# Another written-out order for the steady turns of a two-stream RWKV scan phase: pair products first, transposes between the inversion levels

## The chip, the cores and the metric

The kernel runs on one core of one Trainium2 chip. The metric is the device time of one launch in microseconds (us). In the trace PE is TensorE (matrix multiplies), PEld its weight loads, DVE is VectorE, ACT is ScalarE, POOL is GpSimd, SP is SyncE, which only issues transfers here. A "matmul" below is one MATMUL record of the trace; a float32 product leaves two of them, a transpose leaves one.

## The reference

Two layers of a trunk run over 512 latent and 256 context tokens of width 1024. The part of it that the change touches is the bidirectional RWKV-7 time mixing, for 16 heads of 64 channels and both directions:

```
z = h @ W_in                                   # r, k, v, low-rank decay and rate, gates
k_d, decay_d, kk * a_d  for d in (forward, backward)
for each token (context first, then latent, from the context's final state):
    S = S * w_t - (S @ kk_t) kka_t^T + v_t k_t^T
    y_t = S @ r_t                              # directions are summed
out = (norm(y) + bonus) * g
```

The second layer needs no output for the context tokens, so its scan computes y for 512 tokens only. The convolution branch, the gating unit, the merge and the feed-forward part follow, and the change leaves them alone.

## The kernel before

The scan is computed in chunks of 64 tokens (12 chunks). Two heads, 128 channels, make a pair; there are 8 pairs in each layer. Within a pair, a chunk's step is a set of small products with the inverse of a 64x64 triangular matrix, one for each chunk, head and direction.

`pair_phase(l)` exists once for each engine. It is software-pipelined in turns `t` = 0 to 9 (`KT` is 8). In turn `t` three pairs are in work at once:

* the dense work of pair `t`: the projections of k, r and v (`ktiles`, L1058, 48 products of 128x128 by 512 or 256 columns; half 0 is 512 wide, half 1 is 256 wide), the low-rank decay and rate (`up_group`, L1126, three groups "first", "both", "last") and the norm sums of kk (`single`, L1070);
* the scan of pair `t-1`: `scan(p)` and `side_work(p)`;
* the output part of pair `t-2`: mean, variance, gate (`single`, L1070).

On TensorE the scan of a pair is, in order: six pair products (`product`, 16 matmul records each, PROD0 to PROD5 below), the inversion, the blocks w, u and g, the `sources`, and a chain of 11 hops from chunk to chunk. The inversion has four full levels. Each level n consists of T0, T1, U0 and U1: 96 records of 32x32 each (the helper `mm64`, L1177). A fifth, smaller one follows (L5T, L5U, 96 records each). `side_work` is 13 transposes through TensorE, TR0 to TR12 (`turned`, mostly L1209, four records each).

Between these the other engines work:

* PROD0 waits for `yv`, ScalarE's copy of the previous pair's y out of the same PSUM banks (L2080). That copy also waits for `ya` (L2577, VectorE), since it overwrites what L2577 reads.
* PROD(j) with j >= 2 waits for VectorE's masking (L2618) of product j-2, as there are two pairs of banks.
* When masks 0 to 2 are done ScalarE gathers four blocks, when all six are done four more (L2020). VectorE then makes the start value of the inversion for half 0 and half 1 (L2631, L2634, transpose L2626). L1T0 and L1T1 wait for these.
* ScalarE copies each transpose out (L2001 to L2012, bk0 to bk12 below); transpose k waits for copy k-2.
* After L5T: copies t5 (ACT L2034) and t5v (DVE L2654); after L5U: x5 (ACT L2044) and x5v (DVE L2663). The first block w0 waits for both. Block w1 waits for w0's copy w0st (ACT L2050), since both use one bank; u0 waits for w0's second copy (L2054), u2 and `sources` for the later ones and for u0 to u2 copied out (ACT L2060, DVE L2669).
* ScalarE also computes the next pair's decays and norms in the same turn: kkln (L1924, a logarithm, with a table load L1722 ahead of it), vln0 and vln1 (L1897), kkexp (L1931, an exponential, after another table load), ex0, ex1 (L1939, L1942), ex2, ex3, kt0, kt1 (L1951). On VectorE: the shifts of k, r and v (L2415, L2419), the two running sums sum0 and sum1 (L2512), le (L2523), the factor products (L2397).

The program issues one fixed order of items to each engine. That order comes from `WEAVE`: for each engine, layer and turn there is a string of letters, one letter for one item. `weave(order, **streams)` takes the next item of the stream that each letter names. For TensorE `d` is the dense stream, `s` the scan, `x` the transposes. For ScalarE and VectorE `s` is the scan, `x` the copies of transposes, `t` the tail of earlier pairs, `p` all the rest. Within one stream the order is fixed; only the interleaving is in the string. All steady turns, `t` = 2 to 7 (`range(2, KT)`), of one layer share one string. Since each wait is issued in front of its item, the items behind it on the engine wait too.

SyncE issues the weight loads in its own order (`pair_loads`): each steady turn loads three chunks of 512 KB and one of 192 KB, released when the gate tile of the turn before is done.

Of the kernel before, what the change touches and what calls it, by code (L numbers as in the profile page):

```python
# [37 lines left out]
KT = D // P  # L38
# [109 lines left out]
def names_lora():  # L148
# [20 lines left out]
WEAVE = {}  # L169
# [1 line left out]
    "xxddxdxxdxsdssddddssxxsxdxdddxdxddddsdsddxsddsddsddsdsddsddsddddsdsdssdsddssdsddsdddssdssddddssddsds"  # L171
    "sssssssssssssssssssssssssssssssssssssss")) for t in (1,))
WEAVE.update((("PE", 0, t), (
    "xxdsxsdssdxxssxdxxdddxsddsdddsxddddsdxdddsdsddsddsddsddsxdsddsdddsdddsddsdsdddsdxddsdddsdsdsssssddss"
    "dsssdsssddsdssdssssssssssssssssssssssdsssssss")) for t in range(2, KT))
WEAVE.update((("PE", 0, t), (
    "dxsdsdsxssddxxsxxxdddsxxsxdddsdddddsdddsdddddsddsddddddxddddsdddsxddddssdsdddsssdsxddsdddsddsdsdsdds"
    "sdddssddddsddsssssssddssdsdsssssssssssssssssssssssssssss")) for t in (KT,))
WEAVE.update((("PE", 0, t), "dddddddsddddddddddsddddsddddddddsdddddddddsdddsddddddd") for t in (KT + 1,))
WEAVE.update((("A", 0, t), "xxxxxsspssxxxxssxsspxppppppxppppppppxppspspspssssssssssssspspspsssssss") for t in (1,))  # L180
WEAVE.update((("A", 0, t), "xxxxxsssxsssxssxxppxppxpppppppppxpppssxsppsppspsssspsssppspsppssssspssssss") for t in range(2, KT))
WEAVE.update((("A", 0, t), "sxsxsxsxxxssssxxxpxpppppxxpssxsssssspsssssssssssssssss") for t in (KT,))
WEAVE.update((("A", 0, t), "pxpppxx") for t in (KT + 1,))
WEAVE.update((("V", 0, t), "sssttttsststpssssssssssssspppspspsssspppssssspspsppsstpspsspspspsppppppsppsssssssssssssssssss") for t in (1,))
WEAVE.update((("V", 0, t), "ttssssttsstssstsssstpstsspssssspssspssssppspssppsppsssspssssppppppsppssssptstsssstsssspspstspspsstp") for t in range(2, KT))
WEAVE.update((("V", 0, t), "tsststsststsssssststsssstssspssspspspppssssptstsssppsssssssttsssssssssspsspsppspspspsssspppppp") for t in (KT,))
WEAVE.update((("V", 0, t), "tptppptpttppppppppt") for t in (KT + 1,))
WEAVE.update((("PE", 1, t), (
    "ddddxsdxxssxsddxdssxdxxddddddddsxsdxsddsddsxddsddsdsdsdsssssdsddxddsdsxddddsddssssssddsdssssssdsssss"
    "ssdssssssssssssssssssssssssss")) for t in (1,))  # L190
WEAVE.update((("PE", 1, t), (
    "xxsssdsxssxxdxxddddsxdsdxsddddsddddsddsdxsddsddsddsddxsdsxdsdssdsdsddxsddddsddsdsssddssdsssssdsssdss"
    "ssdddsssssssssssssssssssssssssss")) for t in range(2, KT))
WEAVE.update((("PE", 1, t), (
    "xsssxddxssxxsxddddxsxddsdsdsddsdddddsdssdsdssddddssdddsxsdxxsxsdddxsdddsddssssssssssssssssssssssssss"
    "sssssssssssssssssss")) for t in (KT,))
WEAVE.update((("PE", 1, t), "dddddsdddsddddsdddddddddddd") for t in (KT + 1,))
WEAVE.update((("A", 1, t), "xxxsxsxsspxssxssxpppxpppxppxpppppppppppspsxxsspssssssssssssspssssssss") for t in (1,))
WEAVE.update((("A", 1, t), "xxsssxxxsssssxxxpppxppxppppppppxxpssspxpspppsspssssssppsppspssssssssssps") for t in range(2, KT))
WEAVE.update((("A", 1, t), "xxxsssxsxsxsssxxpppppxxxssxxsssssssssssssssssssssss") for t in (KT,))  # L200
WEAVE.update((("A", 1, t), "pppxxx") for t in (KT + 1,))
WEAVE.update((("V", 1, t), "tssstttsstssssssspsspssppssssppsssspsssppstsspsspspppssspppspspsspppspssspsssssssssssssss") for t in (1,))
WEAVE.update((("V", 1, t), "tssssttstssssssststssspssssspsspspssssspsppsppspspssssssspppppppssssptspssstsssspsspsstspsspt") for t in range(2, KT))
WEAVE.update((("V", 1, t), "stssttsssttssssssssstssssssspspssssstsssstsptsssssspsppsppsssppspsssppsssssspssspspsp") for t in (KT,))
WEAVE.update((("V", 1, t), "ptppptptptppppppppp") for t in (KT + 1,))

# [3120 lines left out]
```

## Time and profile before

| | before |
|---|---|
| median of 3 runs | 4037.71 us (4033.7 to 4046.82) |
| profiled execution: its time | 4042.05 us |
| profiled execution: span of the core | 4040.2 us |
| PE busy | 3832.9 us, 95% of the span |
| DVE, ACT, POOL busy | 1684.2, 1136.4, 552.0 us |
| mean granted TensorE clock | 0.98 |
| scan phase of layer 0, steady turns | 233.45 to 884.36 us, six turns |
| scan phase of layer 1, steady turns | 2459.16 to 3070.76 us, six turns |

Times inside the span are counted from the first instruction. A turn is counted here from the end of the last hop of the pair before to the same point of the next. A timeline row gives the start, the duration, the engine, the source line, the operation, its shapes and the count of instructions merged in it; in brackets stands the idle time before it and what released it. "issue" is idle time in which the engine waited for nothing that the profile shows.

### The profile page before, as it was taken

To read this page: it belongs to the slowest core of one execution; us is meant where nothing else is said; L and a number is where in the kernel's file an instruction comes from. 1 tells how busy PE (TensorE), PEld (TensorE's weight loads), DVE (VectorE), ACT (ScalarE), POOL (GpSimd) and SP (SyncE) were. 2 spreads that over 40 slices of the span, in tenths; PEclk is the share of its full clock that TensorE was granted. 3 is DMA by queue.
4 is the path that set the end of the run, shared out by engine and by line. 5 is a ranking of instruction groups with operands and counts; after the bars stand their busy time and mean duration, and the time that the engine had idled before them with its cause. 6 is when DMAs were issued, how large, how long until landed. Compare 5 with 4: busy or idle time off the path is not lost.

```text
span 4040.2 us, 112746 instructions
## 1 busy us (share of the span) xinstructions
PE 3832.9 (95%) x51864; PEld 2572.9 (64%) x51864; DVE 1684.2 (42%) x2721; ACT 1136.4 (28%) x2003; POOL 552.0 (14%) x436
## 2 busy tenths in 40 slices
PE   7899999999999999999999989999999999999998
PEld 3666666666555555655555656666666556678887
DVE  2656656654872111322231255555555422132232
ACT  3544454542122000200000244444444221020001
POOL 0000000000032121122232100000000023314443
PEclk8999999999999999999999999999999999999999
DMA  5000000000333222211111310000010253242223
GB/s 207 25 9 25 25 25 25 30 18 28 103 134 99 94 94 94 85 52 63 56 59 63 127 42 9 24 24 24 24 34 21 88 187 110 84 143 92 84 91 129
DMA packets 76341, 277.46 MB, mean 69 GB/s; under 512 B 8672, under 2 KB 13024, under 8 KB 75488
## 3 DMA queue, kind: packets, MB, share of 16 engines
q1 hardware_dynamic: 67968, 235.96, 17.6%
q10 hardware_dynamic: 6624, 29.04, 1.9%
q8 instruction: 412, 6.75, 0.7%
q0 software_dynamic: 1280, 5.24, 0.3%
q14 instruction: 57, 0.47, 0.0%
HBM read 256.58 MB, written 13.63 MB: 67 GB/s over the span
## 4 chain that ended last, share of the span: by engine, by line
PE 89%; ACT 4%; issue 3%; DVE 2%; DMA 1%; POOL 0%; ACTq 0%; DVEq 0%; SPq 0%; POOLq 0%
PE psum L1177 17%; PE psum L1691 16%; PE psum L759 11%; PE psum L1058 11%; PE psum L1488 9%; PE psum L1623 6%; PE psum L1583 3%; PE psum L1070 3%; PE psum L1646 2%; PE psum L1209 2%; PE psum L1018 2%; PE psum L750 2%; PE psum L1126 1%; DMA ring<-w_stream_in 1%; PE psum L1036 1%
## 5 line engine op out<-in xcount | busy, mean ns | idle before, releaser
L1177 PEld LDWEIGHTS psum<-arena 32*32 32x32 f32 (+3 forms) x40512 | 702.7, 118 | 366.6 <-issue 281.4
L1177 PE MATMUL psum<-arena 32*32 32x32 f32 (+4 forms) x40512 | 795.4, 209 | 117.5 <-issue 85.1
L1058 PE MATMUL psum<-arena,ring 128*128 128x512 f32 (+1 forms) x1408 | 564.8, 523 | 5.5 <-ACT arena L1879 1.9
L759 PE MATMUL psum<-arena,ring 128*128 128x512 f32 (+1 forms) x1264 | 463.2, 524 | 3.8 <-DVE arena L2577 3.8
L759 PEld LDWEIGHTS psum<-arena,ring 128*128 128x128 f32 x1264 | 238.8, 191 | 230.4 <-issue 200.8
L1691 PE MATMUL psum<-arena 128*128 128x384 f32 (+1 forms) x1344 | 368.6, 433 | 0.0
L1058 PEld LDWEIGHTS psum<-arena,ring 128*128 128x128 f32 x1408 | 243.9, 192 | 133.3 <-issue 105.0
L1691 PEld LDWEIGHTS psum<-arena 128*128 128x128 f32 x1344 | 255.4, 190 | 106.4
L1691 PE MATMUL psum<-arena,ring 128*128 128x384 f32 (+1 forms) x1008 | 278.5, 433 | 0.0
L3016 POOL DMA_DIRECT2D ya_spill<-arena x16 | 8.8, 551 | 1957.5 <-DVE arena L2577 1957.5
L1691 PEld LDWEIGHTS psum<-arena,ring 128*128 128x128 f32 x1008 | 191.5, 190 | 79.6
L2859 DVE TENSOR_TENSOR arena<-psum,arena 128x384 f32<-128x384 f32 (+1 forms) x210 | 99.2, 489 | 309.8 <-PE psum L1691 309.8
L1488 PE MATMUL psum<-arena 128*128 128x384 f32 (+1 forms) x768 | 215.4, 434 | 2.9 <-POOL arena L3053 1.8
L1488 PEld LDWEIGHTS psum<-arena 128*128 128x128 f32 x768 | 145.8, 190 | 65.9 <-issue 4.1
L1488 PE MATMUL psum<-arena,ring 128*128 128x384 f32 (+1 forms) x576 | 169.7, 438 | 14.0 <-DMA ring<-w_stream_in 6.6
L2397 DVE TENSOR_TENSOR arena<-arena 128x768 f32<-128x768 f32 x192 | 175.1, 931 | 10.9 <-ACT arena L1951 5.9
L2380 DVE SCALAR_TENSOR_TENSOR arena<-arena,par 128x255 f32<-128x255 f32 (+18 forms) x296 | 166.3, 595 | 5.3
L2748 DVE TENSOR_TENSOR arena<-psum,arena 128x384 f32<-128x384 f32 (+1 forms) x120 | 56.6, 488 | 252.5 <-PE psum L1488 252.4
L1488 PEld LDWEIGHTS psum<-arena,ring 128*128 128x128 f32 x576 | 108.8, 191 | 67.6 <-issue 6.5
L1827 ACT ACTIVATE arena<-psum 128x512 f32<-128x512 f32 (+1 forms) x88 | 43.7, 497 | 374.9 <-PE psum L1058 374.9
L1722 ACT ACT_TABLE_LOAD x106 | 136.0, 1283 | 34.1 <-DVE arena L2743 20.6
L1623 PE MATMUL psum<-arena 128*128 128x384 f32 (+1 forms) x528 | 145.1, 433 | 0.0
(177 smaller groups left out, 4482.7 us busy)
## 6 DMA issues: line engine op xcount, KB each, us to landing
ring<-w_stream_in SPq DMA_DIRECT2D x440, 512.0 KB, 3.8
x_spill<-arena ACTq DMA_DIRECT2D x2, 3072.0 KB, 8.7
arena<-x_spill ACTq DMA_DIRECT2D x16, 384.0 KB, 6.7
arena<-ya_spill ACTq DMA_DIRECT2D x6, 768.0 KB, 6.0
ring<-w_stream_in ACTq DMA_DIRECT2D x8, 512.0 KB, 5.9
arena<-x_in ACTq DMA_DIRECT2D x1, 3072.0 KB, 14.5
arena<-ups_in SPq DMA_DIRECT2D x16, 192.0 KB, 2.5
ya_spill<-arena POOLq DMA_DIRECT2D x8, 384.0 KB, 5.6
```

What stands on the lines that cost most here:

```text
L759: mm = eng.matmul(psum[0:lhs[k].shape[-1], tile, a - off:b - off], lhsT=lhs[k], rhs=rhs[k][:, a:b], start=(k == 0), stop=(k == len(lhs) - ...
L1058: mm = pe.matmul(bank(j, z=b - a), lhsT=w[k], rhs=hs[k][:, a:b], start=(k == 0), stop=(k == KT - 1))
L1070: pe.matmul(bank(b, z=z - a), lhsT=lhs, rhs=rhs[:, a:z], start=True, stop=True).then_inc(ev.sem, 2 if skip else 1)
L1177: return pe.matmul(out, lhsT=lhs, rhs=rhs, start=start, stop=stop, skip_group_check=True)
L1488: mm = pe.matmul(bank(FREE_BANK[i], z=m), lhsT=left[:, k * P:k * P + P], rhs=right[:, k], start=(k == 0 and i != 2), stop=(k == 3), skip_g ...
L1583: mm = pe.matmul(psum[:, tile, a - c0:b - c0], lhsT=w, rhs=mov[k][:, a:b], start=(k == 0), stop=(k == len(mov) - 1), skip_group_check=True)
L1623: mm = pe.matmul(bank(DOWN_BANK[i], z=m), lhsT=left[:, k * P:k * P + P], rhs=right[:, k], start=((p, i) not in begun and k == 0), stop=(c ...
L1691: mm = pe.matmul(bank(b, z=m), lhsT=left[:, k * P:k * P + P], rhs=right[:, k], start=(k == 0 and i != 2), stop=(k == 3), skip_group_check= ...
L1722: act.add_instruction(mybir.InstLoadActFuncSet(name=nc.get_next_instruction_name(), engine=act.engine, act_func_set_id=n))
L2380: return dve.scalar_tensor_tensor(out=out, in0=in0, scalar=w, in1=out, op0=ALU.mult, op1=ALU.add)
L2397: dve.tensor_tensor(out, a, b, ALU.mult).then_inc(ev.sem, 1)
L2859: dve.tensor_tensor(out, x, y, op).then_inc(*V.mark(name))
```

## The change

Only six of the strings are replaced: TensorE's, ScalarE's and VectorE's for the steady turns of each layer. Every letter count is the same, so the same instructions are issued with the same waits on the same tiles; they stand in another order on their own engine. Turns 0, 1, 8 and 9 and everything outside the scan phases are as before.

```diff
@@ WEAVE, layer 0, t in range(2, KT)
 WEAVE.update((("PE", 0, t), (
-    "xxdsxsdssdxxssxdxxdddxsddsdddsxddddsdxdddsdsddsddsddsddsxdsddsdddsdddsddsdsdddsdxddsdddsdsdsssssddss"
+    "sdssxssxsddxdsddsxddsxdddsdddsxdddsxdddsxdsddxsddsddsddxsdxsdddsdddxsdddsdxsdsdddddddsdsddsdsssdsdss"
     "dsssdsssddsdssdssssssssssssssssssssssdsssssss")) for t in range(2, KT))
...
-WEAVE.update((("A", 0, t), "xxxxxsssxsssxssxxppxppxpppppppppxpppssxsppsppspsssspsssppspsppssssspssssss") for t in range(2, KT))
+WEAVE.update((("A", 0, t), "xssssxssssxpxxpxxpxppxpxpppppxxpxspspspspppppsspssspsssppspsppssssspssssss") for t in range(2, KT))
...
-WEAVE.update((("V", 0, t), "ttssssttsstssstsssstpstsspssssspssspssssppspssppsppsssspssssppppppsppssssptstsssstsssspspstspspsstp") for t in range(2, KT))
+WEAVE.update((("V", 0, t), "ttssssssttssstssssstssstpssptssssppssssssppsspsspssspssssssppppppspppssssppsptssststsssspspstspspsstp") for t in range(2, KT))
@@ WEAVE, layer 1, t in range(2, KT)
-    "xxsssdsxssxxdxxddddsxdsdxsddddsddddsddsdxsddsddsddsddxsdsxdsdssdsdsddxsddddsddsdsssddssdsssssdsssdss"
+    "ssdssxssddxdxsdxsddsdddsxdddsxdddsddxsdsxdsddsddsxddsdxsxdsxddsxsdsddsddddsdsddsdssddssdsssssdsssdss"
     "ssdddsssssssssssssssssssssssssss")) for t in range(2, KT))
...
-WEAVE.update((("A", 1, t), "xxsssxxxsssssxxxpppxppxppppppppxxpssspxpspppsspssssssppsppspssssssssssps") for t in range(2, KT))
+WEAVE.update((("A", 1, t), "xssssxssssxpxpxxpxppxxppxxppppxxpspspspspppsspsspssssppsppspssssssssssps") for t in range(2, KT))
...
-WEAVE.update((("V", 1, t), "tssssttstssssssststssspssssspsspspssssspsppsppspspssssssspppppppssssptspssstsssspsspsstspsspt") for t in range(2, KT))
+WEAVE.update((("V", 1, t), "ttssssssttssstssssssstpsspssssppssssssssppspsppssssssssppppsppsspsppsptpssstsssspsspsstspsspt") for t in range(2, KT))
```

Read through the streams, the parts of the orders that differ are these ("k0.3" is the fourth product of k's half 0):

```
TensorE, layer 0, head and first level
before  TR0 TR1 k0.0 PROD0 TR2 PROD1 k0.1 PROD2 PROD3 mean0 TR3 TR4 PROD4 PROD5 TR5 k0.2 TR6 TR7 k0.3 mean1 k0.4 TR8 L1T0
after   PROD0 k0.0 PROD1 PROD2 TR0 PROD3 PROD4 TR1 PROD5 k0.1 mean0 TR2 k0.2 L1T0
TensorE, layer 1, head and first level
before  TR0 TR1 PROD0 PROD1 PROD2 k0.0 PROD3 TR2 PROD4 PROD5 TR3 TR4 k0.1 TR5 TR6 mean0 k0.2 k0.3 k0.4 L1T0
after   PROD0 PROD1 k0.0 PROD2 PROD3 TR0 PROD4 PROD5 k0.1 mean0 TR1 k0.2 TR2 L1T0
TensorE, layer 1, levels 3 and 4
before  L3T0 r r L3T1 r r TR10 L3U0 up_both L3U1 TR11 norm0 L4T0 norm1 L4T1 L4U0 up_last L4U1 v0.0 L5T v0.1 var0 TR12 L5U v0.2 to v0.5 w0 v0.6 v0.7 w1
after   L3T0 r r L3T1 r r L3U0 TR8 r r L3U1 r TR9 L4T0 TR10 up_both L4T1 TR11 norm0 norm1 L4U0 TR12 L4U1 up_last L5T v0.0 v0.1 L5U var0 v0.2 v0.3 v0.4 w0 v0.5 w1
TensorE, layer 0, end of the levels
before  L4U1 v0.0 v0.1 var0 L5T v0.2 TR12 v0.3 var1 L5U v0.4 v0.5 v0.6 w0 v0.7 w1
after   L4U1 r1.7 TR12 L5T up_last L5U v0.0 v0.1 var0 v0.2 v0.3 var1 v0.4 w0 v0.5 w1
ScalarE, layer 1
before  bk0 bk1 gather x3 bk2 bk3 bk4 gather x5 ...  kkln t5 xd0 xd1 vln0 bk12 kkexp x5 ex0 ex1 kt0 w0st
after   bk0 gather x4 bk1 gather x4 bk2 ...  rg2 t5 rg3 xd0 kkln xd1 vln0 x5 kkexp ex0 ex1 w0st
ScalarE, layer 0, end
before  kkln vln0 t5 xd0 bk12 xd1 vln1 kkexp x5 ex0 ex1 w0st
after   bk12 t5 rg2 xd0 rg3 xd1 kkln x5 vln0 vln1 kkexp ex0 ex1 w0st
VectorE, both layers
the six masks stand together; sum1 and le stand behind x5v; b1 and kd1 behind u2's copy
```

From `sources` on, TensorE's order is the same letter for letter.

## Rows read from the trace of the kernel before

**Rows 1.** The page: engines (busy us, share, count), and the chain that ended last.

```profile
PE 3832.9 (95%) x51864; PEld 2572.9 (64%) x51864; DVE 1684.2 (42%) x2721; ACT 1136.4 (28%) x2003; POOL 552.0 (14%) x436
...
PE 89%; ACT 4%; issue 3%; DVE 2%; DMA 1%; POOL 0%; ACTq 0%; DVEq 0%; SPq 0%; POOLq 0%
```

**Rows 2.** Windows on PE, twelve steady turns: length, busy (count), clock, DMA, GB/s.

```profile
233.45:338.40 104.95, 101.42 (x2778) 1.00 0.02 4
...
772.14:884.36 112.22, 103.85 (x2779) 0.97 0.11 36
...
sum 1262.51, PE 1180.46; mean PE 98.37
```

**Rows 3.** Windows on PE, one turn of layer 0 and of layer 1 by stage.

```profile
338.40:355.32 16.92, 16.92 (x150) 1.00 0.38 125
355.32:406.90 51.58, 48.09 (x1759) 0.97 0.02 4
406.90:425.76 18.86, 17.40 (x447) 1.00 0.01 3
...
2661.18:2676.89 15.71, 15.34 (x141) 1.00 0.05 19
2676.89:2726.16 49.27, 43.23 (x1746) 0.97 0.02 4
2726.16:2745.75 19.59, 18.79 (x445) 1.00 0.01 3
```

**Rows 4.** Timeline of PE within the levels of that layer 1 turn.

```profile
2710.72 0.44 PE L1177 MATMUL psum<-arena 32*32 32x32 f32 x27 [0.74 <-issue]
...
2714.58 0.21 PE L1177 MATMUL psum<-arena 32*32 32x32 f32 x1 [1.04 <-issue]
```

**Rows 5.** The page's DMA queues: packets, MB, share of 16 engines.

```profile
q8 instruction: 412, 6.75, 0.7%
```

**Rows 6.** Windows on PE, from one issue gap's end to the next's.

```profile
2710.72:2714.58 3.86, 2.82 (x129) 1.00 0.02 4
2714.58:2718.42 3.84, 2.02 (x128) 0.95 0.02 4
```

**Rows 7.** Timeline of PE at the head of a layer 0 turn.

```profile
338.40 1.09 PE L1209 MATMUL psum<-const,arena 128*128 128x128 f32 x8
339.33 1.02 PE L1058 MATMUL psum<-arena,ring 128*128 128x512 f32 x2
340.29 1.16 PE L1177 MATMUL psum<-arena 64*128 64x128 f32 x16
```

**Rows 8.** Timeline of ACT and DVE at the head, layers 0 and 1.

```profile
338.51 0.81 ACT L2080 ACTIVATE arena<-psum 128x768 f32<-128x768 f32 x1 [0.68 <-PE psum L1177]
...
2661.98 0.60 ACT L2080 ACTIVATE arena<-psum 128x512 f32<-128x512 f32 x1 [0.76 <-DVE arena L2577]
```

**Rows 9.** Timeline of DVE and ACT from the masks to the first level.

```profile
345.32 2.35 DVE L2618 TENSOR_TENSOR arena<-psum,const 128x1024 f32<-128x1024 f32 x2 [0.92 <-PE psum L1177]
...
2672.10 2.70 ACT L2020 ACTIVATE arena<-arena 32x384 f32<-32x384 f32 x5
...
2673.74 0.56 DVE L2631 TENSOR_TENSOR arena<-arena,const 128x384 f32<-128x384 f32 x1 [1.47 <-ACT arena L2020]
```

**Rows 10.** Timeline of ACT behind the fifth level of a layer 1 turn.

```profile
2725.18 0.84 ACT L1924 ACTIVATE arena<-arena 128x768 f32<-128x768 f32 x1
2726.20 0.80 ACT L2034 ACTIVATE arena<-psum 32x768 f32<-32x768 f32 x1 [0.18 <-PE psum L1177]
...
2729.95 1.28 ACT L1722 ACT_TABLE_LOAD   x1
2731.24 0.94 ACT L1931 ACTIVATE arena<-arena,const 128x768 f32<-128x768 f32 x1
2732.09 0.78 ACT L2044 ACTIVATE arena<-psum 32x768 f32<-32x768 f32 x1
...
2735.39 0.60 ACT L2050 ACTIVATE arena<-psum 128x512 f32<-128x512 f32 x1
```

More of the change, by code:

```diff
@@ L173 @@
 WEAVE.update((("PE", 0, t), (
-    "xxdsxsdssdxxssxdxxdddxsddsdddsxddddsdxdddsdsddsddsddsddsxdsddsdddsdddsddsdsdddsdxddsdddsdsdsssssddss"
+    "sdssxssxsddxdsddsxddsxdddsdddxsdddxsdddxsdsddxsddsddsddxsdxsdddsdddxsdddsdxsdsdddddddsdsddsdsssdsdss"
     "dsssdsssddsdssdssssssssssssssssssssssdsssssss")) for t in range(2, KT))
@@ L184 @@
 WEAVE.update((("V", 0, t), "sssttttsststpssssssssssssspppspspsssspppssssspspsppsstpspsspspspsppppppsppsssssssssssssssssss") for t in (1,))
-WEAVE.update((("V", 0, t), "ttssssttsstssstsssstpstsspssssspssspssssppspssppsppsssspssssppppppsppssssptstsssstsssspspstspspsstp") for t in range(2, KT))
+WEAVE.update((("V", 0, t), "ttssssssttssstsssstssstpssptssssppssssssppsspspssspssssssppppppspppssssppsptssststsssspspstspspsstp") for t in range(2, KT))
 WEAVE.update((("V", 0, t), "tsststsststsssssststsssstssspssspspspppssssptstsssppsssssssttsssssssssspsspsppspspspsssspppppp") for t in (KT,))
```

## The prediction, made before the changed kernel was run

> **What bounds the kernel now.** I read the page first: PE is busy for 95% of the span and carries 89% of the chain that ended last, no other engine half as much [rows 1]. The same instructions are issued after the change, so only TensorE's idle time in the twelve steady turns, and its clock there, can move. These turns are 1262.51 us long and 1180.46 busy [rows 2]: 82 us of idle time is all there is to win, and each new wait of PE adds to the end.
>
> The windows by stage say where it lies. The head (to the start of L1T0) is full: 16.92 of 16.92 us in layer 0, 15.34 of 15.71 in layer 1. The levels (L1T0 to the end of L5T) have 3.5 and 6.0 us idle and a mean clock of 0.97. From there to `sources` 1.5 and 0.8 us are idle [rows 3]. The rest of a turn, unchanged, is 19.7 and 17.0 us (107.05 and 101.53 less the rows).
>
> The timeline calls nearly all idle time in the levels "issue" [rows 4]. I read it as waiting for instructions. The gaps come back after 128 matmuls, 3.86 and 3.84 us apart [rows 6]. The instruction queue moved 6.75 MB in 412 packets [rows 5]; 51864 matmuls with as many weight loads [rows 1] are 252 instructions or 126 matmuls to a packet. So where 128 matmuls take less than about 3.85 us (30.1 ns each), PE outruns its instructions. The levels are such a place: 1746 matmuls in 49.27 us is 28.2 ns, 1759 in 51.58 is 29.3 [rows 3]. With the other stages constant, the levels' mean over the six turns of a layer is 53.0 us in layer 0 (mean turn 108.5, from 104.95 to 112.22 [rows 2]) and 49.7 in layer 1 (mean turn 101.9), that is 30.1 and 28.5 ns for each matmul.
>
> The Trainium skill speaks to this ("Runtime: NRT & Kernel Launch", section "Instruction fetch mechanics"): instructions come in 16 KiB blocks of 256 by the engine's own DMA queue, and the fetch is hidden since dispatch is slower than the fill. The block size agrees with the 252 above; that it is hidden does not agree with a gap every 128 matmuls. What the second half would mean here is the rival "count" below.
>
> **The head.** Removed ahead of L1T0 in layer 0: k0.3, k0.4, mean1 and six transposes. Steps between starts give 0.93 for two transposes, 0.96 for one k product and 1.09 for a pair product [rows 7]; with half of 0.96 for mean1 that is 5.2 to 5.4, leaving 11.5 us of work. Two waits are new.
>
> First, PROD0 now stands first and waits for `yv`. In layer 0 it runs from 338.51 for 0.81 us, to 0.92 after the turn's start; PROD0 can start at 0.98. Until now two transposes and k0.0 covered it. In layer 1 the copy starts only at 2661.98, held by L2577, and ends 1.40 after the turn's start [rows 8]: PROD0 at 1.46.
>
> Second, the chain to L1T0. A mask takes 1.17 us (2.35 for two), a gather 0.54 (2.70 for five), a VectorE step behind them 0.59 (0.56 and a small gap) [rows 9]. Layer 0, counted from the turn's start: PROD0 ends 2.07, PROD5 9.56 (its mask waits all fit within 0.2), the sixth mask 10.9. Two gathers end 12.0, and three VectorE steps (mask, identity, transpose) give L1T0 at 13.9, against 11.5 of work: 2.4 idle. L1T0 came at 16.92, so the head is 3.0 shorter. Before the change four and more items of cover stood between PROD5 and L1T0; now k0.1, mean0, TR2 and k0.2 do, 3.4 us. Layer 1: the sixth mask ends at 10.7, but ScalarE now has bk1 ahead of the second four gathers, and TR1 ends only at 11.75 (behind PROD5, k0.1, mean0). bk1 ends at 12.4, two gathers at 13.4, L1T0 starts at 15.3 with PE ready at 13.25. So 1.46 and 2.0 us idle where 0.37 was; the head is only 0.4 shorter than 15.71.
>
> **The levels.** They get longer in work: layer 0 gains k0.3, k0.4, mean1 and seven transposes (5.8) and gives up_last, v0.0, v0.1 and var0 (3.95) to the tail: +1.85. Layer 1 gains two k products and five transposes and gives v0.0, as written from start to end of L5T: +3.7 less what the 0.5 to 0.55 per transpose leaves uncertain. At full clock the work now is about 47.4 in layer 0, and in layer 1 43.23 busy less 1.5 (a mean of 0.97 is 3.0 us of 49.27 at half clock): 41.7. After: 49.2 and 45.4. These are the floors. The matmuls become 1771 and 1768; at 30.1 and 28.5 ns the instructions need 53.3 and 50.3 us. That is the other bound. Where between? A level step of 96 in 0.95 us needs 2.9 us of instructions, so about 2 us of other work must follow each. Layer 0 now has 2.0 to 3.4 nearly everywhere; short are the places behind L1T0 (1.5), L2U0 (up_first, 1.1), L3U1 and L4U0 (1.6 to 1.7) and L4U1 (1.05), 4.0 us in sum with 0.45 for the 16 matmuls of each up group; the longer ones give some of it back. I take 3.3, so 52.5. Layer 1 still has 1.5 or 1.6 at five places, 1.1 at two, and 0.5 between L4U0 and L4U1: I take the bound, 50.3. Change: -0.5 and +0.6. The clock dips in the rows stand right behind the gaps and lie inside these lengths.
>
> **The tail (L5T's end to `sources`).** ScalarE decides. Now kkln is done before t5 in layer 1, and w0st starts at 2735.39, as w0 ends [rows 10]. After the change the second rate gates, xd0, xd1 and kkln with its table load of 1.28 stand behind t5, then x5, vln0, vln1, another table load, kkexp, ex0, ex1, and only then w0st. Layer 1, from L5U's end: kkln ends 0.7, xd1 1.5, vln0 2.1, x5 2.8, load 4.1, kkexp 5.0, ex0 and ex1 6.4 (0.73 each), w0st 7.0; w0 and v0.5 are done at 5.85, so w1 waits 1.25. Then kt0, kt1 and ex2, ex3 (1.8) push u2st to 17.4 and on VectorE sum1, kk, kq0 push u2's copy to 17.8, so `sources` starts at 17.85, 0.8 late. Layer 0: vln1 waits for var1 at 5.3, the load ends 7.15, w0st 10.1; w1 waits 1.8, `sources` 0.5, at 20.5. From L5T's end that is 23.25 in place of 18.86 (+4.4) and 21.45 in place of 19.59 (+1.9). Before, x5, ex0, ex1 and kt0 took 3.3 together [rows 10], from which the steps of 0.7 to 0.9 here. Queued behind w0st on ScalarE are w0's second copy and all of w1's and u0's, which u0, w2, u1 and u2 wait for; they follow at ScalarE's pace. In layer 1 VectorE has b1, kd1, bq1, ynr and kq1 around the first state copies, so hop 2 and g2 wait 0.25 more.
>
> **Sum.** Layer 0: -3.0 - 0.5 + 4.4 = +0.9 a turn. Layer 1: -0.4 + 0.6 + 1.9 + 0.25 = +2.3. Six turns each: +5 and +14, +19 us. Weight loads keep their order on SP and their release by the gate product; in layer 0 they fall on the head (125 GB/s [rows 3]), where PE needs only 120 to 150 matmuls in 14 us or more, a fraction of what the queue brings, so nothing is priced there. The clock behind the new waits is unknown: between no dip and one like that of a turn's levels, 1.5 us, at most 18 in all. The waits of 1.0 to 2.0 us are about as long as the gaps in the levels, but stand alone between full stretches; I take none, and the upper end for the range. Against the profiled 4042.05 that is 4061; the median is 4.3 lower, so 4056.
>
> **Rivals.** *Instructions no longer short* (the other side: faster). If the evener spacing takes all gaps away, the levels fall to 49.2 and 45.4: layer 0 -3.0 - 3.8 + 4.4 = -2.4, layer 1 -0.4 - 4.3 + 2.15 = -2.55, in all -30: 4008. For it: within layer 0 the other work is now near the 2 us needed, and the turn from 233.45 had 3.5 us idle in all [rows 2]. Against it: layer 1's 0.5 and 1.1 slots, and a count that grows. It decides once the levels fall below 51.6 in layer 0 and 48.0 in layer 1. *Half of it*, or a tail that ScalarE does not hold up: with levels at 51.3 and 47.9, layer 0 is -0.3 and layer 1 -0.1 a turn, 4035; without the waits of w1 and `sources`, it is -1.4 and +0.25, 4031. No measurable change. *Count*: the gaps belong to the small matmuls, whose number is unchanged, and not to their spacing. Then the excess of 5.6 and 8.0 us stays on top of the longer work: levels 54.8 and 53.4, layer 0 +3.2, layer 1 +5.4, 4090.
> The page's sentence on hidden fetch, taken alone, gives this rival.
>
> **How the numbers follow.** Forecast (4046 to 4072) 0.45; count 0.07; half or no ScalarE wait 0.28; instructions no longer short 0.20. 0.3%, 12 us, is about what a measurement of this kernel can tell from no change. Nearly all of the first two is above it: slower 0.50, same 0.29, faster 0.21. The range takes the forecast and the half case whole and half of each outer case, which leaves out some 2 in 10 with what is unforeseen: 4018 to 4084. The likeliest case alone has 4046 to 4072, its upper end from the clock.
>
> **What would show it.** Right if, in the changed profile, PE starts a turn with 1.0 and 1.4 us idle released by L2080; L1T0 stands 13.9 and 15.3 us into the turn; the levels last 52 to 53 and about 50 us with "issue" gaps still there in layer 1; and PE waits for L2050 before w1 by 1.2 to 1.8 us. Wrong if the levels' idle time (3.5 and 6.0 us in the turns of rows 3) shrinks to under 1 us, if the wait on L2050 is missing, or if the granted clock in turns falls for longer behind the new waits at the head, which this sum doesn't price.

## The result

The changed kernel takes 4088.49 us (median of 4 runs, 4078.97 to 4097.25), the kernel before 4042.01 us beside it (4 runs, 4033.7 to 4046.82). The ratio is 1.0108, with a 95% interval from 1.0088 to 1.0129: slower by 46 us. The prediction said 4056, in a range of 4018 to 4084; the direction came true, the growth is more than twice the 18 us that it means, and the time lies outside the range. The profiled execution took 4092.22 us with a span of 4090.4, at a mean granted clock of 0.979.

Page of the changed kernel: engines, instruction queue, and the chain that ended last. Instructions, matmuls and packets are those of before [rows 1, 5]; in the chain PE has 87% instead of 89%, and ScalarE, VectorE and issue each have one more.

```profile
PE 3848.7 (94%) x51864; PEld 2579.7 (63%) x51864; DVE 1690.8 (41%) x2721; ACT 1141.2 (28%) x2003; POOL 550.8 (13%) x436
...
q8 instruction: 412, 6.75, 0.7%
...
PE 87%; ACT 5%; issue 4%; DVE 3%; DMA 1%; POOL 0%; ACTq 0%; DVEq 0%; SPq 0%; POOLq 0%
```

Windows on PE, two of the twelve steady turns and their sum. Against [rows 2] the turns are 52.0 us longer (1314.52 less 1262.51); PE's busy time grows by 16.6 of that, so 35.4 is idle time.

```profile
563.32:676.12 112.80, 105.65 (x2778) 0.95 0.07 22
...
2585.27:2692.81 107.54, 97.38 (x2698) 0.95 0.07 22
...
sum 1314.52, PE 1197.07; mean PE 99.76
```

Windows on PE, one turn of each layer by stage (head, levels, tail), to be read against [rows 3]. The last of the first three shows the granted clock at 0.82 over 28 us, in a tail that was at 1.00 before; the head of layer 1 is at 0.90. In other turns of this trace layer 0's tail takes 23.74 us at 1.00, and layer 1's head 14.99.

```profile
563.32:577.11 13.79, 11.88 (x119) 1.00 0.44 153
577.11:628.23 51.12, 48.89 (x1771) 1.00 0.02 4
628.23:656.42 28.19, 25.45 (x462) 0.82 0.01 2
2585.27:2601.89 16.62, 12.95 (x120) 0.90 0.05 18
2601.89:2652.17 50.28, 46.48 (x1767) 0.97 0.02 4
2652.17:2675.35 23.18, 21.32 (x446) 0.92 0.01 3
```

Timeline of PE at the head of that layer 1 turn, the place of [rows 7 to 9]. The first pair product waits 1.39 us for ScalarE's copy, L1T0 2.28 us for VectorE. Between them stands the half clock: two pair products (x32) take 2.96 us and then 2.00, one k product 1.84 us and then 1.02. (In the first of the six turns PROD0's wait is only 0.69 us, in each trace of this order.)

```profile
2586.73 2.96 PE L1177 MATMUL psum<-arena 64*128 64x64 f32 x32 [1.39 <-ACT arena L2080]
2589.61 1.84 PE L1058 MATMUL psum<-arena,ring 128*128 128x512 f32 x2
2591.39 2.00 PE L1177 MATMUL psum<-arena 64*128 64x128 f32 x32
...
2598.15 1.02 PE L1058 MATMUL psum<-arena,ring 128*128 128x512 f32 x2
...
2601.89 0.51 PE L1177 MATMUL psum<-arena 32*32 32x32 f32 x36 [2.28 <-DVE arena L2626]
```

The same wait ahead of L1T0 in the turn before. Here it is followed by half clock: the 96 small products take 1.50 us instead of 1.02, the k product 2.08 instead of 1.13.

```profile
2492.05 1.50 PE L1177 MATMUL psum<-arena 32*32 32x32 f32 x96 [2.28 <-DVE arena L2626]
2493.49 2.08 PE L1058 MATMUL psum<-arena,ring 128*128 128x512 f32 x2
```

Timeline of PE in layer 0's tail. v products that take 1.02 us at full clock take 1.88 at half; behind them w1 waits 1.75 us for ScalarE. In this turn the half clock stands ahead of this wait, behind issue gaps of 0.69 and 0.41 us.

```profile
627.68 0.62 PE L1177 MATMUL psum<-arena 32*32 32x32 f32 x26 [0.69 <-issue]
628.24 1.93 PE L1126 MATMUL psum<-arena 64*128 64x128 f32 x16
630.10 2.45 PE L1177 MATMUL psum<-arena 32*32 32x32 f32 x84
632.95 0.53 PE L1177 MATMUL psum<-arena 32*32 32x32 f32 x12 [0.41 <-issue]
633.42 3.78 PE L1058 MATMUL psum<-arena,ring 128*128 128x512 f32 x4
...
645.76 1.16 PE L1177 MATMUL psum<-arena 64*64 64x64 f32 x64 [1.75 <-ACT arena L2050]
```

In the turn before, it stands behind the wait: two v products take 3.38 us where two at full clock take 1.98.

```profile
531.32 1.16 PE L1177 MATMUL psum<-arena 64*64 64x64 f32 x64 [1.75 <-ACT arena L2050]
532.41 3.38 PE L1058 MATMUL psum<-arena,ring 128*128 128x512 f32 x4
```

The four traces of this order have 14 pieces of half clock in their 24 tails of layer 0: eight begin ahead of w1's wait, 0.2 to 5.3 us behind an issue gap, six begin within 1.6 us behind the wait's end.

Timeline of ACT in layer 1's tail, to be read against [rows 10]. vln0 (L1897) waits for PE's var0, the table load behind it starts 7.97 us after the end of L5T (2652.17) where it started 3.79 after it before, and the copy of w0 (L2050), behind both exponentials, comes 11.58 us after it, 9.23 before.

```profile
2658.76 0.69 ACT L1897 ACTIVATE arena<-psum,const 128x512 f32<-128x512 f32 x1 [1.22 <-PE psum L1070]
2659.34 0.78 ACT L2044 ACTIVATE arena<-psum 32x768 f32<-32x768 f32 x1
2660.14 1.28 ACT L1722 ACT_TABLE_LOAD   x1
2661.44 0.94 ACT L1931 ACTIVATE arena<-arena,const 128x768 f32<-128x768 f32 x1
2662.28 0.83 ACT L1939 ACTIVATE arena<-arena 128x768 f32<-128x768 f32 x1
2663.02 0.82 ACT L1942 ACTIVATE arena<-arena 128x768 f32<-128x768 f32 x1
2663.75 0.57 ACT L2050 ACTIVATE arena<-psum 128x512 f32<-128x512 f32 x1
```

**Where the time went, over several traces.** One trace is not enough here: the same order differs by up to 2 us a turn between profiled executions. So I took every trace of the steady turns of either order, and sorted PE's time in a mean turn four ways: *gaps* are idle time that the timeline calls issue, *waits* idle time released by another engine, *clock* is each stage's length times one less its granted clock, and *work* what is left of the busy time. (The windows give the clock to two places, so a stage of 50 us is good to some 0.25. The wait at a turn's end is counted in both neighbours, 0.2 us and 0.3 in the last row; idle time too short for the timeline is in none of the terms. They add up to the turn within 0.2.) The order of before has four traces for each layer (the first, two repeats, and runs that leave that layer alone), the changed order four for layer 0 and three for layer 1.

| mean turn, us | turn | gaps | waits | clock | work |
|---|---|---|---|---|---|
| layer 0, before | 107.87 | 4.14 | 1.98 | 0.82 | 100.96 |
| layer 0, changed | 110.09 | 2.87 | 4.91 | 1.21 | 101.10 |
| layer 1, before | 101.83 | 5.41 | 1.53 | 3.20 | 91.54 |
| layer 1, changed | 107.61 | 4.18 | 6.62 | 4.10 | 92.71 |

A pair of turns grows by 8.0 us, six pairs by 48, which is the result. New waits are 8.0 a pair (2.93 and 5.09; 7.9 without what is counted twice); the gaps give back 2.5; the clock takes 1.3 and work 1.3.

### The profile page after: what moved, and what is told of

Same layout as the page of the kernel before. It is cut to its first block, busy times and chain, and to the rows that moved or that the text cites. A ratio compares the mean times of both kernels' runs of the same rounds, so it can differ in the third digit from the quotient of the medians.

```text
span 4090.4 us, 112746 instructions
## 1 busy us (share of the span) xinstructions
PE 3848.7 (94%) x51864; PEld 2579.7 (63%) x51864; DVE 1690.8 (41%) x2721; ACT 1141.2 (28%) x2003; POOL 550.8 (13%) x436
## 4 chain that ended last, share of the span: by engine, by line
PE 87%; ACT 5%; issue 4%; DVE 3%; DMA 1%; POOL 0%; ACTq 0%; DVEq 0%; SPq 0%; POOLq 0%
PE psum L1177 17%; PE psum L1691 15%; PE psum L759 11%; PE psum L1058 11%; PE psum L1488 9%; PE psum L1623 6%; PE psum L1583 3%; PE psum L1646 2%; PE psum L1209 2%; PE psum L1070 2%; PE psum L750 2%; PE psum L1018 2%; PE psum L1126 1%; DMA ring<-w_stream_in 1%; PE psum L1036 1%
## 5 line engine op out<-in xcount | busy, mean ns | idle before, releaser
L1177 PE MATMUL psum<-arena 32*32 32x32 f32 (+4 forms) x40512 | 805.1, 209 | 157.9 <-issue 76.9
L1058 PE MATMUL psum<-arena,ring 128*128 128x512 f32 (+1 forms) x1408 | 578.3, 531 | 3.6 <-ACT arena L1879 1.3
L759 PE MATMUL psum<-arena,ring 128*128 128x512 f32 (+1 forms) x1264 | 463.1, 524 | 3.8 <-DVE arena L2577 3.8
L2647 DVE TENSOR_TENSOR arena<-arena,psum 128x384 f32<-128x384 f32 x128 | 70.7, 553 | 195.6 <-PE psum L1177 195.5
```

The source lines that it names most:

```text
L759: mm = eng.matmul(psum[0:lhs[k].shape[-1], tile, a - off:b - off], lhsT=lhs[k], rhs=rhs[k][:, a:b], start=(k == 0), stop=(k == len(lhs) - ...
L1058: mm = pe.matmul(bank(j, z=b - a), lhsT=w[k], rhs=hs[k][:, a:b], start=(k == 0), stop=(k == KT - 1))
L1177: return pe.matmul(out, lhsT=lhs, rhs=rhs, start=start, stop=stop, skip_group_check=True)
```

## The experiments

A diff in operation names shows an order of the steady turns that is a string of letters in the code. "Ratio" is always to the kernel before, measured beside it. Where turns are given, they are means of six in one trace.

**One layer alone.** Layer 0's three strings changed, layer 1's as before.

```diff
 WEAVE.update((("PE", 1, t), (
-    "ssdssxssddxdxsdxsddsdddsxdddsxdddsddxsdsxdsddsddsxddsdxsxdsxddsxsdsddsddddsdsddsdssddssdsssssdsssdss"
+    "xxsssdsxssxxdxxddddsxdsdxsddddsddddsddsdxsddsddsddsddxsdsxdsdssdsdsddxsddddsddsdsssddssdsssssdsssdss"
...
```

> Only layer 0's steady strings are the new ones. If the two layers' losses are independent, as the stages of the two traces say (mean steady turn of layer 0 108.5 before and 111.5 after), this kernel is 18 us slower than before, and the other 34 us belong to layer 1. If instead the order in layer 0 moves something that layer 1 inherits (the phase of the instruction fetch), it is not 18 but anywhere between 0 and 50.

Measured: 4049.24 us, ratio 1.0039 (1.0024 to 1.0053), 4031.11 before beside it: 18 us. Layer 0's turn is 109.78, layer 1's 101.77. So less than half of the loss is layer 0's; the other 28 us are layer 1's, to which the prediction gave 14. (The mean turns of the table give 13 and 35.)

**The tail's wait.** ScalarE's copies of w0 ahead of the exponentials, in the changed kernel, both layers.

```diff
-kkexp ex0 ex1 w0st w0z kt0
+kkexp w0st w0z ex0 ex1 kt0
```

> The changed kernel with w0's two copies (w0st, w0z) ahead of ex0 and ex1 on ScalarE. Theory A (ScalarE holds w1 up, and that wait is an additive loss): PE's wait for L2050 goes from 1.75 and 1.0 to 1.6 us to under 0.3, and the steady turns shorten by 1.3 to 1.8 us, 15 to 20 us in all. Theory B (the wait also brings the half clock of the tail): the dips in the tails vanish too, 30 to 38 us in all. Theory C (ex0 and ex1 come late and the wait reappears at sources or a hop): under 5 us.

Measured: 4073.77 us, ratio 1.0101 (1.0069 to 1.0134), where the changed kernel has 1.0108. In the trace the waits in the tails fall from 2.4 to 1.3 us in layer 0 and from 2.2 to 0.9 in layer 1, and the turns are 108.45 and 106.52 (changed: 110.09 and 107.61, so 16 us less in all); the times show only some 3 us, in an interval that reaches from no gain to 16 us. The waits are real and about a third of the new ones; their worth in the whole time is not settled by this run. The stages show why it is small. Layer 0's tail is 1.8 us shorter, and all six are at full clock. Layer 1's is no shorter (22.5 us): where its wait was, PE now has an issue gap of 0.87 to 1.14 us, and what layer 1's turn gained stands in the clock of its heads (0.57 us lost, 1.52 in the changed kernel), which this edit does not touch.

**The head's first wait.** Two transposes ahead of the first pair product, in the changed kernel, both layers.

```diff
-PROD0 k0.0 PROD1 PROD2 TR0 PROD3 PROD4 TR1 PROD5        (layer 0)
+TR0 TR1 PROD0 k0.0 PROD1 PROD2 PROD3 PROD4 PROD5
-PROD0 PROD1 k0.0 PROD2 PROD3 TR0 PROD4 PROD5 k0.1 mean0 TR1 k0.2        (layer 1)
+TR0 TR1 PROD0 PROD1 k0.0 PROD2 PROD3 PROD4 PROD5 k0.1 mean0 k0.2
```

> The changed kernel with TR0 and TR1 back ahead of PROD0 on TensorE. Theory A (the loss at the head is an uncovered wait for yv, and in layer 1 bk1 holding up the gathers): L1T0 comes 0.7 us earlier in layer 0 and 1.7 earlier in layer 1 in the turn, and the levels have two transposes less to hold only if L1T0 is not delayed; together 12 to 15 us faster than the changed kernel, and the clock dips at layer 1's heads (1.6 us each in three turns) go with the waits, another 5. Rival (the levels are bound by their instructions, so an earlier start of L1T0 only means a fuller wait there): under 5 us.

Measured: 4059.93 us, ratio 1.0061 (1.004 to 1.0083): nearly half of the loss is gone, about as much as expected with the clock's share. It is all in layer 1: head 13.42 (16.29), levels 49.71 (51.19), turn 103.30. Layer 0's stays at 109.65, for its head was set by the later wait for VectorE. In layer 1 this edit shortens two waits, not one, since TR1, whose copy stood ahead of the gathers, moves too: PROD0's falls from 1.39 to 0.37 us, L1T0's from 2.28 to 1.24, and one of 0.49 behind a mask is new. That is 1.4 us a turn less of waits; the gaps stay, and the clock takes 3.3 less (0.8 us a turn where it was 4.10). So three quarters of layer 1's gain is half clock that went with the waits. Its heads are at full clock in all six turns; this window is one of them.

```profile
2571.00:2584.49 13.49, 11.40 (x119) 1.00 0.06 22
```

**The head's first wait, alone.** The kernel before, with its first pair product moved ahead of what covered it. Nothing else moves.

```diff
-TR0 TR1 k0.0 PROD0 TR2 PROD1        (layer 0)
+PROD0 TR0 TR1 k0.0 TR2 PROD1
-TR0 TR1 PROD0 PROD1                 (layer 1)
+PROD0 TR0 TR1 PROD1
```

> The kernel before with one step moved in its steady turns: the first pair product stands first, ahead of the transposes and the k product that covered the copy it waits for. Theory A, a wait costs its length: PROD0 waits 0.9 us at the turn's start in layer 0 and 1.4 in layer 1 (0.37 before), heads at 17.9 and 16.7 us, clock of the head at 1.00, 6 + 6 us in all, less what the fetch gaps of the levels give back. Theory B, that such a wait ahead of full work brings the half clock: a granted clock of 0.90 or so in heads of layer 1, another 1 to 1.6 us a turn, 20 us or more in all.

Measured: 4053.21 us, ratio 1.0047 (1.0029 to 1.0064), 19 us. Windows on PE of three heads of this kernel, two of layer 1 and one of layer 0:

```profile
2664.16:2680.93 16.77, 15.38 (x140) 1.00 0.04 17
2767.73:2786.09 18.36, 16.97 (x141) 0.91 0.04 16
660.19:677.93 17.74, 16.84 (x150) 1.00 0.32 120
```

And the timeline of PE in the second: behind the wait of 1.39 us, two pair products take 3.40 us where two take 2.06 a little later.

```profile
2769.19 1.11 PE L1177 MATMUL psum<-arena 64*128 64x64 f32 x16 [1.39 <-ACT arena L2080]
2770.23 1.33 PE L1209 MATMUL psum<-const,arena 128*128 128x128 f32 x8
2771.49 3.40 PE L1177 MATMUL psum<-arena 64*128 64x128 f32 x32
...
2777.51 2.06 PE L1177 MATMUL psum<-arena 64*128 64x128 f32 x32
```

In layer 0 the wait of 0.90 us costs nothing that one trace can show (the four of before differ by 1.1 us a turn): heads 0.8 longer, levels 0.7 shorter, turn 107.97 (107.87). In layer 1 four of six heads are at 0.90 or 0.91 (before: 1.00 in all of 24), and the turn is 104.51 (101.83): waits +1.04, clock +1.10, gaps +0.22, work +0.28. A wait of 1 us cost 2.7. The length of the wait does not decide it alone: one of the four is the first turn, whose wait is 0.69 us, and two turns with 1.39 keep full clock. Theory B holds for layer 1 and theory A, with its payback, for layer 0.

**A wait in the tail, alone.** The kernel before, ScalarE's copies of w0, w1 and u0 behind both kt operations.

```diff
-ex0 ex1 w0st kt0 w0z w1st w1z u0st kt1        (layer 0)
+ex0 ex1 kt0 kt1 w0st w0z w1st w1z u0st
-ex0 ex1 kt0 w0st w0z kt1 w1st w1z u0st        (layer 1)
+ex0 ex1 kt0 kt1 w0st w0z w1st w1z u0st
```

> The kernel before, with ScalarE's copies w0, w1 and u0 moved behind both kt operations in every steady turn, so that TensorE waits at w1 in the tail with nothing else changed. Theory A, a wait costs its own length: the wait for ScalarE at w1 grows by about 1.7 us in layer 0 and 1 in layer 1, part of it taken back at u0, tails 1 to 1.7 us longer, granted clock of tail and rest at 1.00 as before, 12 to 18 us in all. Theory B, that added waits of this size bring the half clock: the tail's granted clock falls to 0.9 or less in some turns, as in the changed kernel, and the kernel is 25 us or more slower.

Measured: 4037.29 us, ratio 1.0011 (1.0 to 1.0023), 4 us. Layer 0's tail is 19.31 (18.84) with 0.4 us more of waits: w1 waits 1.12 us, and most of it is taken back at u0. Layer 1's does not change. All tails are at 1.00. So the waits that I expected (1.7 and 1) were too long, and one of 1.12 us at this place brings no half clock; one of 1.75, as in the changed kernel, was not run alone.

**The crowded end of the levels.** The changed kernel, with layer 0's first two v products ahead of L5U.

```diff
-up_last L5U v0.0 v0.1 var0
+up_last v0.0 v0.1 L5U var0
```

> The changed kernel, with layer 0's first two v products (steady turns) moved from behind L5U to ahead of it. Theory, that layer 0's half clock and the issue gaps in the tail come from the run of short stages L4U1, L5T, up_last, L5U, with no wide product between them and a wait behind: the tail's granted clock rises from 0.92 to about 1.0 and its issue idle goes, 1.5 to 2 us a turn, 9 to 12 us in all. Rival, that the half clock comes of the wait for ScalarE at w1 or of the wide products themselves: tail unchanged within 0.5 us a turn.

Measured: 4079.5 us, ratio 1.011 (1.009 to 1.0131); the changed kernel beside it 1.0114. The gaps of layer 0's tail do go (0.72 to 0.07 us), its clock is 0.988, but a new wait of 0.77 us for ScalarE (L1890) takes their place, and the tail is 24.60 us. The work was only moved in front of a wait that something else sets.

**The changed kernel twice more, and before once more.** For the scatter.

> The changed kernel once more, on the chip of this group of runs, so that the others can be compared with it here: 4085 us, ratio to before 1.008 to 1.013, and the same stage means (layer 0: 13.8, 51.9, 26.1, 19.7; layer 1: 16.0, 51.6, 22.5, 17.6).

Measured: 4083.35 us, ratio 1.0114 (1.0085 to 1.0143); turns 109.71 and 107.84.

> The changed kernel a third time, for the scatter of the clock between profiled executions. If the half clock belongs to the order: lost clock of 0.8 to 2.3 us a turn in layer 0, all in the tail, and 3.4 to 4.4 in layer 1, half of it in the head. If it is chance: heads of layer 1 at 1.00 in this trace, or lost clock in layer 0's levels.

Measured: 4074.38 us in one execution; turns 109.38 and 107.39. Clock 0.87 a turn in layer 0, all in the tail, and 4.49 in layer 1, 1.7 of it in the heads (four of six at 0.81 or 0.90).

> The kernel before once more. If the half clock belongs to the order: heads and tails of both layers at 0.99 to 1.00, lost clock of 0.3 to 1.1 us a turn in layer 0 and 2.6 to 3.3 in layer 1, nearly all in the levels. If it is chance, some in a head or tail.

Measured: 4036.1 us in one execution; turns 107.51 and 101.88; layer 0's heads and tails and layer 1's heads at 1.00, layer 1's tails at 0.988, clock 0.82 and 3.32 a turn. So the place of the half clock belongs to the order; how much of it falls there varies: 0.8 to 2.3 us in layer 0's turns.

**Fetch or count.** Two kernels made TensorE's instruction stream longer. (A third was to do so with empty instructions; they were not in the program, whose instruction count of 112746 was unchanged. It ran at ratio 1.0003, from 0.9987 to 1.002, and served as a repeat of before.)

> The kernel before, with 8 empty instructions behind each projection product of the scan phases (5632 in all); no other work is changed. Theory A (the issue gaps are TensorE waiting for its instructions, about 15 ns for each): in the levels stand 29 such products in layer 0 and 20 in layer 1, so the levels get 3.5 and 2.4 us longer, about 35 us in the steady turns, with longer issue gaps, and the other stages, which have instructions to spare, stay within 0.5 us. The instruction queue moves some 22 packets more. Theory B (the gaps belong to the small matmuls and their number): levels unchanged.

Eight semaphore increments behind each product:

```diff
                         yield
+                        for _ in range(8):
+                            settle(pe)
```

> The kernel before, with eight more semaphore increments on TensorE behind each projection product (26 to 28 products a steady turn lie in the levels' stretch). They compute nothing; they only make TensorE's instruction stream longer. Theory A, that the idle gaps of the levels are the arrival of instructions: about 15 ns for each added instruction, 3.5 us a steady turn more in layer 0's levels (53.0 to 56.5) and 2.4 in layer 1's (49.8 to 52.2), more packets in the queue q8 (412 before), some 35 to 60 us over the kernel with the other phases. Theory B, that the gaps follow the small matmuls themselves: levels and packets unchanged but for what an increment costs the queue of TensorE, and that cost would then show in every stretch, the tail with its wide products too (tail of layer 0 at 18.8 us if it costs nothing).

Measured: 4282.13 us, ratio 1.0611 (1.0583 to 1.0639). The page counts 118378 instructions, 5632 more, and 22 more packets. But the increments have a price of their own: a pause stands in front of nearly every product or stage that follows them, in layer 0's tail and rest too (issue idle 0.97 and 1.22 us a turn, which were 0 to 0.06). The timeline of PE in the levels:

```profile
416.08 1.01 PE L1179 MATMUL psum<-arena 32*32 32x32 f32 x96 [0.54 <-issue]
417.02 0.70 PE L1058 MATMUL psum<-arena,ring 128*128 128x256 f32 x2
418.21 0.63 PE L1211 MATMUL psum<-const,arena 128*128 128x128 f32 x4 [0.49 <-issue]
```

The time tells nothing between the theories; the packets count 256 instructions each. So the second one cut the products into pieces:

```diff
-mm = pe.matmul(bank(j, z=b - a), lhsT=w[k], rhs=hs[k][:, a:b], start=(k == 0), stop=(k == KT - 1))
+for c in range(0, b - a, 128):
+    mm = pe.matmul(bank(j, z=b - a)[:, c:c + 128], lhsT=w[k], rhs=hs[k][:, a + c:a + c + 128], start=(k == 0 and c == 0), stop=(k == KT - 1 and c == b - a - 128))
```

> The kernel before, with every projection product issued in pieces of 128 columns instead of 512 or 256 at once: the same columns and the same result, more matmul instructions. If each 256 instructions of TensorE come as one packet of q8, the 704 products add 5632 instructions and 22 packets (412 to 434). Theory A, fetch: the levels grow by about 15 ns for each instruction added in them (some 280 in layer 0: 4.2 us a turn, as issue idle), while the tail, with its wide products and slack, grows less. Theory B, that small matmuls alone bring the gaps: issue idle in the levels stays at 4.4 and 5.4 us a turn and only the products' own busy time can change.

Measured: 4059.43 us, ratio 1.006 (1.0046 to 1.0074). Page of this kernel:

```profile
span 4060.8 us, 118634 instructions
...
q8 instruction: 435, 7.13, 0.7%
```

5888 more instructions and 23 more packets: again 256 each. Layer 0's levels hold 111 more matmuls and take 53.19 us where the order of before has 52.39 (mean of four); their gaps are 4.47 (4.14), their work is 0.9 larger. In layer 1 it is 87 matmuls, 50.26 and 49.66 us. Theory A asked for 4.2 us of idle time in layer 0; the levels grew by 0.8 (1.3 at equal clock), the gaps by 0.3. The gaps are tied to packets (in this kernel too most come 127 or 128 matmuls apart, as in [rows 6], or twice that), but instructions did not arrive at a fixed rate that bounds the levels as a whole.

**Putting the good parts together.** The changed order at the head, its early products and spread transposes between the levels (not letter for letter), the order of before at the end.

```diff
-PROD0 k0.0 PROD1 PROD2 TR0        (layer 0, from the changed kernel)
+TR0 TR1 PROD0 k0.0 PROD1
...
-L4U1 r1.7 TR12 L5T up_last L5U v0.0 v0.1 var0
+up_last L4U1 v0.0 v0.1 var0 L5T v0.2 TR12 v0.3 var1 L5U
```

> The changed order at the head and between the levels (pair products early, transposes spread, though the first two stand ahead of the first product), and the order of before behind the fifth level: ScalarE's exponentials and VectorE's sums early again, the first v products ahead of the fifth level's second product. If the changed kernel's loss is all in its head (wait on the masks) and its tail (wait on ScalarE, half clock, bunched stages), and its early products and spread transposes cost nothing or help: layer 0 at 13.6 + 52 + 18.9 + 19.7 = 104.2 us a steady turn (108.5 before), layer 1 at 13.4 + 50 + 19.6 + 16.9 = 99.9 (101.9 before), some 35 us faster than before. Rival, that the work between levels, not its order at the ends, makes the loss: the levels lengthen by what the head gives back, 57 and 52 us, and the kernel is level with before.

Measured: 4046.53 us, ratio 1.0037 (1.0023 to 1.0051). Layer 1's turn is 100.66, 1.2 better than before (head 13.43, levels 51.04, tail 19.28), near what I expected. Layer 0's is 111.04, 7 worse than expected: levels 58.88. In my sum I left out that up_last, v0.0, v0.1 and var0 (3.95 us) stay in the levels in this order; and a wait of the r products on ScalarE's sigmoid (L1879) is new. Timeline of PE, in the levels of the turn that starts at 341.47:

```profile
379.24 3.41 PE L1058 MATMUL psum<-arena,ring 128*128 128x512 f32 x4 [2.33 <-ACT arena L1879]
```

The rival stands for layer 0, whose levels are longer still than its 57, the theory for layer 1. Two more, both with VectorE's v shifts and centring moved behind the first diagonal blocks:

```diff
-mask5 vsh1a vsh1b xf0 xi0 xt0.0 cen0 xf1 xi1 xt0.1
+mask5 xf0 xi0 xt0.0 xf1 xi1 xt0.1 vsh1a vsh1b cen0
```

> Both layers' steady turns in an order put together from what the runs showed. Layer 0: the changed order, with the first two transposes ahead of the first product, ScalarE's w0 copies ahead of its two exponentials, and VectorE's two v shifts and its centring behind the first diagonal blocks. Layer 1: the order of the hybrid kernel (products early, transposes spread, the end of before) with the same three VectorE operations moved. If waits and clock add up as the separate runs show: layer 0 at 12.7 + 51.3 + 23.7 + 19.7 = 107.4 us a turn (108.5 before), layer 1 at 12.5 + 51.0 + 19.3 + 16.9 = 99.7 (101.9 before), 20 us faster than before, ratio 0.995. Rival, that VectorE is late at the next level instead: the wait moves from L1T0 to L1T1 and layer 0 stays at 108.4, layer 1 at 100.7, ratio 0.998.

Measured: 4045.43 us, ratio 1.0028 (1.0018 to 1.0037). Layer 0's turn 110.09, layer 1's 101.52. L1T0 did not come earlier (13.61 us into the turn, as in the kernel with only the transposes moved). Timeline of DVE in this kernel, at a head of layer 0: the first step behind the masks waits for ScalarE's gathers, which had hidden the two shifts.

```profile
460.09 1.22 DVE L2618 TENSOR_TENSOR arena<-psum,const 128x1024 f32<-128x1024 f32 x1
462.45 0.56 DVE L2631 TENSOR_TENSOR arena<-arena,const 128x384 f32<-128x384 f32 x1 [1.13 <-ACT arena L2020]
```

The shifts then made VectorE late in the levels (waits there 1.41 us, 0.2 in the changed kernel), and two of six tails of layer 0 were 28 and 26.5 us, at 0.88 and 0.94. The rival is nearer, and too kind.

> Before in layer 0; in layer 1 the order of the hybrid kernel with VectorE's two v shifts and its centring behind the first diagonal blocks. Layer 1 at 99.7 us a turn (101.9 before), or 100.7 if VectorE's wait only moves on to the next level; layer 0 unchanged. 8 to 13 us faster than before, ratio 0.997 to 0.998.

Measured: 4026.07 us (10 runs, 4020.07 to 4033.98), ratio 0.9982 (0.9973 to 0.9991), before 4033.5 beside it. Layer 1's turn is 100.79, layer 0's 107.42 in the old order. This is the fastest kernel of the study, 7 us ahead of before: less than the 0.3% taken as the bound, but with an interval that excludes no change. Windows on PE of its six turns of layer 1:

```profile
sum 604.73, PE 558.75; mean PE 93.13
```

## Why the prediction was right in direction and too small

Its stages, against the mean of the traces of the changed order (us a turn; work, waits and clock together):

| stage | predicted, layer 0 | measured | predicted, layer 1 | measured |
|---|---|---|---|---|
| head | 13.9 | 13.80 | 15.3 | 16.29 |
| levels | 52.5 | 51.19 | 50.3 | 51.19 |
| tail | 23.25 | 25.41 | 21.45 | 22.58 |
| rest | 19.7 | 19.70 | 17.25 | 17.55 |

**The waits: right.** PROD0 waits 0.90 and 1.39 us at the turn's start (forecast 0.98 and 1.46 after it); L1T0 1.01 and 2.28 (1.4 and 2.0); w1 1.75 and 0.99 to 1.59 (1.8 and 1.25), released by the line that was named. Summed up, the prediction's new waits are 2.4 and 3.1 us in the heads, 1.0 and 1.25 in the tails and 0.25 in the rest, 8.0 a pair of turns; measured 8.0. By place it is less exact: in the heads 1.9 and 3.2 were measured, behind the levels 1.1 and 2.0 (forecast 1.0 and 1.5), and 0.4 of old waits in the levels went. That they are the loss, the head kernel shows for the head's two waits in layer 1: with them 1.4 us a turn shorter nearly half of the loss is gone, most of it half clock. For the tail's wait no time shows it.

**The clock: this step failed.** "The clock behind the new waits is unknown ... I take none." In the three stages priced as if at full clock the traces lose 1.21 us a turn (layer 0's tail), 1.52 and 0.94 (layer 1's head and tail), together 3.7 a pair or 22 us. The stages above miss by 4.05 a pair, 24 us, and the turns of before's first trace, from which the sum started, were 0.7 a pair longer than its four traces' mean, 4 us more. That is nearly all of the 32 us between 4056 and 4088. The prediction had written down up to 18 us for this and left it out of the sum; its own sign of being wrong, a longer fall of the clock behind the new waits at the head, is what came. By where the half clock begins, 2.8 us a pair (17 us in all) stand in or right behind a new wait: 1.52 at PROD0 and 0.85 at L1T0 (nine of 18 turns) in layer 1, 0.43 at w1 in layer 0. The other 0.78 of layer 0's tail begins ahead of w1, behind issue gaps, 0.7 us a turn of them, which the sum had at nothing too. Layer 1's tail has the end of a dip that begins near the end of its levels, as before. The reason given, that the waits are about as long as the gaps and stand alone between full stretches, is refuted by the moved pair product: such a wait, alone, in front of full work, brought the half clock to four heads of six in layer 1. It did so in no head of layer 0.

Read by where it was, the clock looks worse than it is: over all stages it cost only 1.3 us a pair more than before (layer 0 0.82 to 1.21, layer 1 3.20 to 4.10), for much of the half clock left the levels. Layer 0's levels lost about 0.8 us a turn to it and now lose none, and they are 1.3 us shorter than forecast. So the half clock largely moved from the levels, whose forecast length included it, to the head and tail, whose forecast did not.

**The levels and the gaps: right in size, doubtful in reason.** 102.4 us of levels a pair were measured where 102.8 were forecast, and the gaps gave back 2.5 us a pair, in both layers. But the bound of 30.1 and 28.5 ns for each matmul, read as the arrival of instructions, didn't hold when matmuls were added (split). Layer 1's levels were 0.9 over it. The gaps fell with the same instructions in another order, from 4.14 to 2.87 and from 5.41 to 4.18, so they depend on what stands where a packet ends; the rival "count", with levels of 54.8 and 53.4, did not come true. That it forecast 4090 is chance. The Trainium skill ("Runtime: NRT & Kernel Launch", section "Instruction fetch mechanics") gives 256 instructions to a block, as both longer kernels show exactly (5632 for 22, 5888 for 23); its statement that the fetch is hidden agrees with neither kernel's gaps, but the price of a further packet in the steady turns (1.9 us a pair of turns for nearly 3 of them) is far below the 3.85 us that stand between two gaps.

**Open.** Layer 1's work grew by 1.17 us a turn with the same matmuls at the same clock; finer alternation of kinds of matmul is a guess that no run tested. What brings the half clock to layer 0's tail isn't settled: issue gaps and w1's wait of 1.75 us each stand ahead of some of it. A wait of 1.12 us at w1 alone doesn't bring it; without the gaps (0.988) it was less, and with w1's wait down to 0.29 it was gone in one kernel (1.000) and there in another (0.970). Why a wait of 0.90 us does nothing in layer 0's head and those of 0.69 and 1.39 do in layer 1's, not each time, is open too.

## What to carry to other kernels

Count what stands between an instruction and the one that it waits for, and keep it there: here 1 us of uncovered wait at the start of a full stretch cost 2.7 us in one layer and nothing in the other (one trace), so price such a wait at up to three times its length. Where a cover is taken away from one step and spread over others, put the new waits at full price and of the gaps expect little back: 2.5 of 9.6 us a pair here. Before a sum starts from a trace, take a second one: in layer 0 two executions of one order lay as far apart (2.1 us a turn) as the two orders.

## What the runs showed of the chip that I had not expected

- One instruction packet is exactly 256 instructions of TensorE: 5632 more gave 22 packets, 5888 gave 23. Added instructions did not cost the 3.85 us a packet that the spacing of the gaps suggests.
- Semaphore increments are not free for TensorE: 5632 of them cost 248 us, 44 ns each, three times the 15 ns that I had reckoned with.
- Half clock in the middle of a stretch without idle time: in layer 1's heads of the kernel with the moved product, behind a wait of 1.39 us, two pair products take 3.40 us instead of 2.06. The same wait brings nothing in two of the six turns, and one of 0.69 us brings it in the first.
